# Two chunk splits and the layers' input norm sum moved earlier in a two-part transformer kernel

## The reference, cut to what matters

```python
for l in range(DEPTH):                       # first block, 272 tokens
    h = h + 0.5 * swiglu(rms_norm(h, ffn1_norm[l]), ffn1_w_gu[l], ffn1_w_down[l])
    u = rms_norm(h, mix_norm[l])
    ...                                      # latent attention and a gated recurrence
    h = h + merged @ w_out[l]
    h = h + 0.5 * swiglu(rms_norm(h, ffn2_norm[l]), ffn2_w_gu[l], ffn2_w_down[l])
return rms_norm(h, final_norm)[:, N_META:]
...
def macaron_ffn(x, pre_g, post_g, w_gate, w_up, w_down):     # second block, 256 tokens
    h = swiglu_2(rms_norm_2(x, pre_g), w_gate, w_up, w_down)
    return x + MACARON_WEIGHT * rms_norm_2(h, post_g)
```

## Time and profile before

| | |
|---|---|
| Time, median of 3 runs | 2539.19 us (2535.57 to 2542.91) |
| Profiled execution | 2541.36 us, its span 2539.2 us |
| PE busy | 2379.8 us (94% of the span) |
| DVE busy | 1423.7 us (56%) |
| ACT busy | 1177.5 us (46%) |
| POOL busy | 606.0 us (24%) |
| Granted TensorE clock, mean | 0.959 of full speed |

### The profile page before, as it was taken

How to read it: one execution, slowest core, us unless ns; L and a number is a source line. 1 busy time by engine, 2 the same in 40 slices (tenths; PEclk the granted TensorE clock), 3 DMA queues, 4 the chain that set the end, 5 groups by cost and what they waited for, 6 DMA issues and landing times.

```text
span 2539.2 us, 50458 instructions
## 1 busy us (share of the span) xinstructions
PE 2379.8 (94%) x18338; PEld 2302.9 (91%) x18338; DVE 1423.7 (56%) x1950; ACT 1177.5 (46%) x1754; POOL 606.0 (24%) x623
## 2 busy tenths in 40 slices
PE   7999889999999999899999989986899999988998
PEld 6999886799999999877899989986899999987998
DVE  5556763455555556744655556467564655455553
ACT  4445532344434436432444345456554445445453
POOL 4221220033213211300332233123432122111420
PEclk9999997899999999988999999998999999988999
DMA  5554222245544544221355535533455465532553
GB/s 194 179 185 156 99 98 86 88 138 190 182 158 159 191 156 149 82 86 59 125 167 180 175 130 193 196 119 125 133 198 193 141 214 186 194 126 72 185 199 108
DMA packets 99268, 380.29 MB, mean 150 GB/s; under 512 B 10911, under 2 KB 13087, under 8 KB 99144
## 3 DMA queue, kind: packets, MB, share of 16 engines
q1 hardware_dynamic: 99144, 378.63, 44.2%
HBM read 377.52 MB, written 3.16 MB: 150 GB/s over the span
## 4 chain that ended last, share of the span: by engine, by line
PE 61%; issue 26%; POOL 4%; DVE 3%; ACT 2%; POOLq 2%; DVEq 1%; DMA 0%; ACTq 0%; SPq 0%
PE bank L563 19%; PE bank L565 19%; PE bank L564 19%; POOL kd L1946 1%; POOLq L1893 1%; PE bank L624 1%; DVE wlo L1344 1%; PE bank L626 1%; PE bank L625 1%; POOL midlo L1954 1%; ACT whi L960 1%; POOL z L1913 0%; PE bank L581 0%; POOLq L1881 0%; DVE cv L1674 0%
## 5 line engine op out<-in xcount | busy, mean ns | idle before, releaser
L1344 DVE TENSOR_TENSOR wlo<-raw,whi 128x1024 fp32r<-128x1024 f32 (+1 forms) x660 | 879.8, 1344 | 535.6 <-ACT whi L960 534.5
L563 PE MATMUL bank<-xhi,wlo 128*128 128x272 f32 (+1 forms) x3392 | 988.7, 291 | 20.0 <-DVE wlo L1344 16.3
L565 PE MATMUL bank<-xhi,whi 128*128 128x272 f32 (+1 forms) x3392 | 982.1, 290 | 0.0
L564 PE MATMUL bank<-xlo,whi 128*128 128x272 f32 (+1 forms) x3392 | 982.1, 290 | 0.0
L960 ACT ACTIVATE whi<-raw 128x1024 fp32r<-128x1024 f32 (+1 forms) x660 | 729.2, 1118 | 505.6 <-PE bank L565 474.2
L563 PEld LDWEIGHTS bank<-xhi,wlo 128*128 128x128 f32 x3392 | 655.1, 193 | 25.3 <-issue 22.4
L565 PEld LDWEIGHTS bank<-xhi,whi 128*128 128x128 f32 x3392 | 653.6, 193 | 0.0
L564 PEld LDWEIGHTS bank<-xlo,whi 128*128 128x128 f32 x3392 | 652.3, 192 | 0.0
L563 PE MATMUL bank<-hidhi,wlo 128*128 128x272 f32 (+1 forms) x1408 | 400.5, 284 | 0.0
L565 PE MATMUL bank<-hidhi,whi 128*128 128x272 f32 (+1 forms) x1408 | 399.5, 284 | 0.0
L564 PE MATMUL bank<-hidlo,whi 128*128 128x272 f32 (+1 forms) x1408 | 399.3, 284 | 0.0
(11 more groups left out here) (315 smaller groups left out, 2704.7 us busy)
## 6 DMA issues: line engine op xcount, KB each, us to landing
raw<-ffn_gu SPq DMA_DIRECT2D x352, 512.0 KB, 3.5
raw<-ffn_down SPq DMA_DIRECT2D x128, 704.0 KB, 4.1
raw<-mix SPq DMA_DIRECT2D x120, 512.0 KB, 3.5
raw<-rec SPq DMA_DIRECT2D x28, 512.0 KB, 3.7
raw<-kv SPq DMA_DIRECT2D x16, 512.0 KB, 4.2
raw<-att SPq DMA_DIRECT2D x16, 512.0 KB, 4.4
bias_rows<-rows SPq DMA_DIRECT2D x8, 256.0 KB, 4.3
bias<-bias_rows SPq DMA_DIRECT2D x1, 1536.0 KB, 9.3
```

The lines of the kernel that those rows point to most:

```text
L563: pe.matmul(out, wlo[:, slot, w], xh(i), start=(i == 0), stop=False)
L564: pe.matmul(out, whi[:, slot, w], xl(i), start=False, stop=False)
L565: mm = pe.matmul(out, whi[:, slot, w], xh(i), start=False, stop=(i == last))
L1344: dve.tensor_tensor(wlo[:, k, 0:cols], raw[:, k, 0:cols], whi[:, k, 0:cols].bitcast(F32), ALU.subtract).then_inc(lo_made, 1)
```

## The change

Three things move; nothing is added to or taken from what is computed.

1. In the layers' FFNs (F0 to F3) PE does `norm_sum` behind tile 3 in place of tile 4, and `norm_back` behind tile 4 in place of tile 5. ACT's root and DVE's reciprocal go in front of the split of tile 7's chunk (`k == 3`).
2. In the seven stages of the second half the split of tile 8's chunk goes in front of the root (ACT) and of the reciprocal (DVE). F6 has no norm of its own.
3. There, too, the split of tile 9's chunk goes behind `norm_copy` on ACT, in front of all work on tiles 0 to 3, and on DVE behind the emptying of tile 3's bank.

The second quad of ACT's FFN is written out of the loop for this. The diff, cut to its core (KV and ATT are changed as REC is). PE:

```diff
                     k8_tile(q + t // RING, t % RING, j + 4 if t == 7 else None, early_bank(t), (xhi, xlo), c)
-                    if t == 4 and main_norm:
+                    if t == (4 if c else 3) and main_norm:
                         input_norm(x, n, c)()
-                    if t == 5 and main_norm:
+                    if t == (5 if c else 4) and main_norm:
                         norm_back(n, c)
```

ACT, with the recurrent stage's loop last:

```diff
             def first_splits(q, j, n, c, main_norm=True):
                 for k in range(RING):
+                    if k == 3 and main_norm and c == 0:
+                        norm_std(n, c)
                     split_hi(q + 1, k, CH8, j + k + 1)
+                if c:
+                    split_hi(q + 2, 0, CH8, j + 5)
+                    if main_norm:
+                        norm_std(n, c)
                 if main_norm:
-                    norm_std(n, c)
                     norm_copy(n, c)
+                if c:
+                    split_hi(q + 2, 1, CH8, j + 6)
...
-                def quad(b, next_cols, first=False):
+                def quad(b, next_cols, first=False, begun=False):
...
-                        if not first:
+                        split = not first and not (begun and p == 0)
+                        if split:
                             split_hi(b + q + 1, 2 * p, next_cols, tile + 1)
...
                 quad(0, CH8, first=True)
-                with act.Fori(1, FFN_GU_QUADS - 1) as b:
+                quad(1, CH8, begun=c > 0)
+                with act.Fori(2, FFN_GU_QUADS - 1) as b:
...
                 for t in range(16):
-                    if t >= RING:
+                    if t >= RING + 2:
                         split_hi(q + 1 + t // RING, t % RING, CH8, j + t + 1)
```

DVE, with the recurrent stage's loop last:

```diff
             def first_splits(q, n, c, main_norm=True):
                 for k in range(RING):
+                    if k == 3 and main_norm and c == 0:
+                        norm_inv(n, c)
                     split_lo(q + 1, k, CH8)
+                if c:
+                    split_lo(q + 2, 0, CH8)
+                    if main_norm:
+                        norm_inv(n, c)
                 if main_norm:
-                    norm_inv(n, c)
                     dve.wait_ge(rstd_made, rstd_copies(n))
...
                 quad(0, CH8, first=True)
-                quad(1, CH8, banks=(4, 5, 6, 3))
+                if c:
+                    split_lo(q + 2, 1, CH8)
+                quad(1, CH8, begun=c > 0, banks=(4, 5, 6, 3))
...
-                    if RING <= t < 16:
+                    if t == RING - 1:
+                        split_lo(q + 2, 1, CH8)
+                    elif RING + 2 <= t < 16:
                         split_lo(q + 1 + t // RING, t % RING, CH8)
```

More of the change, by code:

```diff
@@ L1263, in attention @@
                 first_splits(q, j, n, c)
-                for t in range(RING, 8):
+                for t in range(RING + 2, 8):
                     split_hi(q + 1 + t // RING, t % RING, CH8, j + t + 1)
@@ L1359, in first_splits, with quad @@
                 for k in range(RING):
+                    if k == 3 and main_norm and c == 0:
+                        norm_inv(n, c)
                     split_lo(q + 1, k, CH8)
+                if c:
+                    split_lo(q + 2, 0, CH8)
+                    if main_norm:
+                        norm_inv(n, c)
                 if main_norm:
-                    norm_inv(n, c)
                     dve.wait_ge(rstd_made, rstd_copies(n))
             def ffn(q, j, x, n, f, c, main_norm=True):
-                def quad(b, next_cols, first=False, banks=(0, 1, 2, 3)):
+                def quad(b, next_cols, first=False, begun=False, banks=(0, 1, 2, 3)):
                     if first:
@@ L1730, in keys_values @@
                         x_lo(11, t, c)
-                    if t >= RING:
+                    if t == RING - 1:
+                        split_lo(q + 2, 1, CH8)
+                    elif t >= RING + 2:
                         split_lo(q + 1 + t // RING, t % RING, CH8)
```

## The result

The changed kernel takes 2517.56 us, the median of 4 runs (2511.02 to 2521.63), beside 2540.74 for the kernel before on the same chip (2535.57 to 2542.91). The ratio is 0.9909, with a 95% interval of 0.9882 to 0.9937: 23.2 us less, between 16.0 and 30.0 by the interval, against 22.7 forecast. The profiled execution took 2521.63 us, with a span of 2519.5 us.

What follows compares the result with a forecast made beforehand. PE, busy 94% of the span, was taken as the bound. Gains of 15.7 (layers), 7.3 (F4, F5, F7) and 0.6 (REC) less 0.95 (KV) made 22.7 us: 2541.36 to 2518.7, as median 2517, range 2510 to 2526.

Steps and rivals of the forecast that it cites:

- What bounds, and what ends the hole: PE bounds; its tile 8 holes in seven FFNs come from late splits, the norm waiting only for PE's order.
- Part 1, 15.7 us: F0 to F3: norm one tile earlier closes tile 8's hole and restores the clock, 4 x 3.93 us gained.
- the clock falls all the same: Rival in F0 to F3: sum and back still bring half speed, giving back 6.5 us, 2523; chance 0.14.
- full clock over the first 30 us of F2: Sign of being right: granted clock 1.00 over the first 30 us of F1, F2 and F3.
- Part 2: Second half: tile 8's split before the norm, weights 9 us early; back's cover 1.0 us in F5, 0.6 F4, 0.7 ATT.
- one of the signs that the prediction named as wrong: Second half: a wait of PE on `inv` would show the prediction wrong.
- the new wait on the norm's way: Rival, second half: root and reciprocal wait for a late chunk; 3.8 us in each of six stages cancels the gain; chance 0.02.
- Part 3 and the second half, 7.3 us: F4, F5, F7: with tile 9's split behind `rstd`, the holes close, gaining 3 x 2.44 us.
- No clock comes back, as it was at 1.00: F4, F5, F7: closing the holes recovers only their length, the clock behind them having been full already.
- F6, REC, KV: Tile 9's earlier split: F6 costs 0, at most 0.5 us; REC gains 0.6; KV loses 0.95 at tile 7.
- ATT, "nothing changes": ATT: nothing waited at tile 8 before, so no change in time was claimed.
- The mixers: Stages where half-speed stretches come and go, counted as scatter in the range; the runs' spread was 7 us.

Runs made afterwards that it cites:

- Part 1 alone: The layers' norm sum and back moved one tile earlier, second half left as before, against the kernel before: 2529.18 us, ratio 0.9948.
- parts 2 and 3 alone: Splits of tiles 8 and 9 moved earlier in the second half, layers left as before, against the kernel before: 2529.51 us, ratio 0.9949.

## Why the prediction was right, and where it wasn't

The mechanism came out as forecast, and so did the size of its largest term. That the median is within 0.5 us of the forecast is in part luck: the interval of the gain is 14 us wide, the two profiled executions are 19.7 us apart, and one term of the second half was taken from a single execution.

**What bounds, and what ends the hole: right.** Part 1 alone closes the four holes of the layers and parts 2 and 3 alone the three of the second half. That PE's order was all that held the norm up in the layers is shown by the run that moves PE's places only.

**Part 1, 15.7 us: right in mechanism and size.** F0 to F3 lost 15.4 us in two profiles (815.0 for 830.4). In the profile of the result they lost 12.6 only. The missing 2.8 lie at the end of F1, where PE stood 3.85 us before the first matmul of F2 for 2.42 before, and in a half-speed stretch behind that (below). Neither follows from the change: four other profiles with the layers so changed have 815.0 us within 0.1, and a fifth, where only the half-speed stretch is there, 816.1. The clock did come back with the hole, so the rival "the clock falls all the same" is out: no half-speed stretch in F0 and F1, where there were 3.4 us in each. Of the signs that it named, full clock over the first 30 us of F2 failed in the profile of the result, for the reason just given.

**Part 2: right, but for ATT.** 1.1 us of cover at F5's back for 1.0 forecast, 0.66 for 0.6 in F4, and no wait at tile 8. In ATT 0.7 was forecast, from a chunk that lands before tile 4's end; there the `whi` of tile 8 had to wait for its chunk in six of the ten profiles with part 2. The cover was 0.1 us in the profile of the result, and in the two further profiles of the changed kernel PE waited 0.25 and 0.29 us for `inv`, one of the signs that the prediction named as wrong. ACT and PE in the first of these two:

```profile
2245.41 1.06 ACT L960 ACTIVATE whi<-raw 128x1024 fp32r<-128x1024 f32 x1 [2.78 <-DMA raw<-att]
...
2247.86 0.71 PE L581 MATMUL bank<-consts,inv 128*128 128x128 f32 x4 [0.25 <-DVE inv L1359]
```

So the rival "the new wait on the norm's way" is real, at 0.3 us in one stage and not the 3.8 us in six that would cancel the gain.

**Part 3 and the second half, 7.3 us: the mechanism right, one term probably too small, one attribution wrong.** The profiled pair agrees with the number, 598.4 to 591.0, 7.4 us. But the step "No clock comes back, as it was at 1.00" was read off one execution. The same holes cost 1.7 us more each in the profile with part 1 alone, and the trace of the kernel before had a warning that 256 columns don't keep the clock up: behind five other gaps of 2.33 to 2.35 us it falls (see the last section). What the change is worth there may be up to 3 x 4.1 = 12.4 us; parts 2 and 3 alone gained 10.9 to 13.0. How often half speed followed these holes in the kernel before is not known: only one execution of it was profiled. The sum for the median is then between 22.7 and 27.8, and the three measurements of the changed kernel give 23 to 26. And the prediction let tile 9's early split have a share in closing the holes; without it they stay closed.

**F6, REC, KV: right.** F6 192.1 as before. REC 0.5 us less for 0.6 forecast. KV's tile 7 stands idle for 1.38 us, 0.94 more than in the earlier trace rows, for 0.95 forecast; the stage is 0.7 longer, as 0.5 us less of it is at half clock. The wait in the changed kernel:

```profile
2008.13 0.36 PE L563 MATMUL bank<-midhi,wlo 128*128 128x256 f32 x1 [1.38 <-DVE k L1747]
```

**ATT, "nothing changes": wrong, and not settled.** It takes 90.1, 88.4 and 88.5 us in three profiles of the changed kernel, 91.9 in the one of before, with 21, 16 and 16 us at half clock for 27. The runs don't say that the change does it: with parts 2 and 3 alone it takes 91.9, with part 1 alone 90.7, and in both profiles with tile 9's split later in KV, which leaves ATT itself as changed, 91.9 and 91.8. Inside ATT one wait of PE fell from 1.0 to 0.5 us (for `q`) and the next rose from 3.0 to 3.5 (for `sc`), which is nothing in sum. The six profiles in which tile 8's chunk came late there have 88.3 to 90.1 us, the three others with ATT as changed 91.8 to 91.9. What sets it was not found.

**The mixers.** The prediction gave them no change and some scatter. They gave 637.0, 640.2 and 631.8 us for 634.8: up to 5.4 more and 3.1 less. That is most of the range of the runs (12 us over 16 executions), and why a variant that should be 1 us faster can't be told from one that isn't.

## What to carry to other kernels

When a weight chunk is late, follow it back through the engines' lists to the first wait that is not needed. In the layers that led from DVE and ACT to one small step of PE that stood a tile too late, and moving PE's steps alone closed the holes. The price of an idle time on TensorE is its length and what the clock does behind it; one profiled execution doesn't tell the second part, so take it from several places or several executions, and put both values in the range. A split moved from behind the work to in front of it has to be looked at in every stage that shares the code: what is free in an FFN was 0.9 us of idle time in KV. And a step put behind a chunk's landing has to be looked at where the chunk lands latest, as in ATT.

## What was not expected of the hardware

**The same idle time, with and without the fall of the clock.** Holes of 2.15 to 2.31 us in front of dense work were followed by a granted clock between 0.50 and 0.74 in 10 of 14 cases: four of four in F0 to F3 of the kernel before, three of four with parts 2 and 3 alone, none of three in F4, F5, F7 of before and all of three with part 1 alone. The same stage and the same length come with both. The Trainium skill, in "TensorE: Matmul & The Clock Gate", section "HAM oscillation — how this bites in real kernels", has the clock fall behind longer gaps than these; these rows show it behind 2.15 us, though not each time.

The place does matter. PE is also idle at the start of a stage, and there the same length gives a fall always or nearly never. Two of these places in the kernel before, F5 and F2:

```profile
1802.19 0.40 PE L624 MATMUL bank<-xhi,wlo 128*128 128x256 f32 x1 [2.33 <-DVE xlo L1355]
...
1802.19:1805.10 2.91, 2.91 (x14) 2.91 (x15) 2.81 (x6) 1.76 (x5) 0.00 (x0) 0.53 0.00 0
...
749.23 0.39 PE L624 MATMUL bank<-xhi,wlo 128*128 128x272 f32 x1 [2.42 <-DVE xlo L1355]
...
749.23:752.26 3.03, 3.03 (x24) 3.03 (x25) 2.20 (x2) 1.90 (x2) 0.00 (x0) 1.00 0.26 53
```

At the starts of REC, F5, KV, ATT and F7 the gap is 2.33 to 2.36 us in all twelve profiles, and half speed follows in 60 of 60. In front of F2 it is 2.27 to 2.70 us in nine of them, and half speed follows in one. What sets the two kinds apart was not tried.

**The end of the layers' loop.** Between F1 and F2 PE branches back to the loop's start. The first matmul of F2 in the changed kernel and, in a second execution of it, the same, each with the `xlo` of DVE that it needs, and the clock of the stretch behind it:

```profile
733.63 2.35 DVE L1353 TENSOR_TENSOR wlo<-raw,whi 128x1024 fp32r<-128x1024 f32 x2
...
740.82 0.50 DVE L1364 SCALAR_TENSOR_TENSOR xlo<-h,vec,xhi 128x272 fp32r<-128x272 f32 x1 [0.81 <-ACT xhi L992]
...
743.38 0.39 PE L624 MATMUL bank<-xhi,wlo 128*128 128x272 f32 x1 [3.85 <-DVE wlo L1353]
...
743.38:747.60 4.22, 4.22 (x21) 4.22 (x22) 0.77 (x1) 1.04 (x1) 0.00 (x0) 0.60 0.68 223
```

```profile
741.07 0.50 DVE L1364 SCALAR_TENSOR_TENSOR xlo<-h,vec,xhi 128x272 fp32r<-128x272 f32 x1 [0.81 <-ACT xhi L992]
...
742.12 0.39 PE L624 MATMUL bank<-xhi,wlo 128*128 128x272 f32 x1 [2.34 <-DVE xlo L1364]
...
742.12:746.30 4.18, 4.18 (x33) 4.18 (x34) 2.28 (x2) 1.98 (x2) 0.07 (x1) 1.00 0.44 133
```

The `wlo` that the first names as releaser had been done since 735.98, and `xlo` at 741.32, so by the trace PE waited for no other engine. Its record of PE's branch lasts 5.47 us there and 4.03 in the second, and ends 0.4 us before the first matmul of F2 in both. Over the profiled executions that have it as changed or part of it, it lasted 3.9 to 4.4 us in seven and 5.3 to 5.5 in three, the same code each time. F2 had a half-speed stretch behind all three long ones, and behind one of the others. It costs 1.4 us and 1.5 more with the clock, in some executions and not in others; what makes the branch long was not tried.

**The mixers' clock.** M0 and M1 took between 630.4 and 640.2 us in twelve profiled executions, with 99 and 137 us of them at half clock. It is the largest scatter in this kernel, about 0.3 us for each us at half clock (an estimate, a line through the twelve), and no change here reached it.
